# Ranking, placing and gathering the first expert's rows by row blocks, with the Exp table load behind the first weight slots, in a two-layer hybrid decoder trunk

## The chip, the cores and the metric

The kernel runs on one core of a Trainium2 chip. The metric is the device time of one execution in microseconds (us), taken as the median of several runs. Five engines work from queues of their own and wait for each other through semaphores: TensorE (PE, matmuls; PEld its weight loads), VectorE (DVE), ScalarE (ACT), GpSimd (POOL) and SyncE (SP, which here only issues the loads of weights).

## The reference, cut to what matters

```python
def rms_norm(x, g):
    xf = x.astype(jnp.float32)
    y = xf * lax.rsqrt(jnp.mean(xf * xf, axis=-1, keepdims=True) + NORM_EPS)
    return (y * g.astype(jnp.float32)).astype(x.dtype)

def moe_swiglu(h, w_router, w_gate, w_up, w_down):
    B, S, D = h.shape                      # 1, 256, 1024
    t = h.reshape(-1, D)
    logits = (t @ w_router).astype(jnp.float32)
    top_v, top_i = lax.top_k(logits, TOP_K)    # 2 of 8 experts
    top_w = jax.nn.softmax(top_v, axis=-1)
    combine = jnp.sum(jax.nn.one_hot(top_i, N_EXPERTS, dtype=jnp.float32) * top_w[..., None], axis=1)
    out = jnp.zeros_like(t)
    for e in range(N_EXPERTS):
        y = (jax.nn.silu(t @ w_gate[e]) * (t @ w_up[e])) @ w_down[e]
        out = out + combine[:, e:e + 1].astype(t.dtype) * y
    return out.reshape(B, S, D)

# each of two layers: x += concat(attention(h), conv(h)) @ w_out with h = rms_norm(x),
# then layer 0: x += dense_swiglu(rms_norm(x)), layer 1: x += moe_swiglu(rms_norm(x))
```

All data is float32. The sequence has 256 rows of 1024 numbers, an expert is 3584 wide.

## The kernel before

**Weights.** Every weight matrix is streamed in slots of 128 x 2048 numbers (1 MB). SP loads a slot into one of six buffers `raw`; ScalarE copies it to `w_high` in a shorter float format (`high(s)`), VectorE computes `w_low = raw - w_high` (`low(s)`), and TensorE multiplies in three terms (high by high, high by low, low by high; `terms`). `w_high` and `w_low` have three buffers each. So `high(s)` waits until slot s - 3 is used (`w_used`), and SP's load of slot s waits until the low part of slot s - 6 is done. The order of all this on each engine is written out by hand; there is no planner. An engine works strictly in that order.

**Rows.** The 256 rows are two blocks of 128 (NB = 2; b = 0, 1). `xr` holds them. `ps` is the accumulation memory, eight banks of 128 x 512.

**From layer 1's output projection to the first expert.** The last projection leaves its result in banks 4 to 7. VectorE adds it to `xr` in four halves (`add_rows`, counted by `x_added`), TensorE turns the rows (`turn_early`, `turn_rest`), ScalarE and VectorE copy the turned rows to `hT_plain` (`hT_plain_done`), and ScalarE squares the rows for the norm (`norm(3, (), split=False)`; `rms_done`). TensorE multiplies the turned rows with the router (`router(0, S)`, `router(1, P)`; four groups of columns side by side, whose sum is then made by `mm(..., lgT, mask)`), the rest of block 1 with plain matmuls, and signals `summed`. In `route` VectorE reads the logits (`lg`), compares every expert with every other (`cmp_a`), counts (`rank`) and picks the best two (`sel`, `sel_done`). TensorE counts by matmuls with a triangle (`tri`) and ones (`counted`). VectorE makes the place of each row (`possel`) and a one-hot tile `onehot[:, b, 0]` scaled with the row's norm factor (`onehot_done`). TensorE's `gather_first` multiplies `xr` with it: expert 0's rows come out turned, in banks 2, 3, 6 and 5. ScalarE copies them with the gain (`xg[0]`, `first_high_done`, L974), VectorE makes the low part in `first_low` (L1253). Then `gate_up(S_MOE, ...)` begins: slots 0 and 1 (counted from `S_MOE`) are the gate, 2 and 3 the up projection of 512 columns; slots 4 and 5 are the next columns' gate.

`fill(n, bank)` issues n matmuls of a zero tile whose results nobody reads. GpSimd's `list_tokens` makes the difference of the two best logits (`zdiff_done`), whose `Exp` gives the weights of the sum; they are read only in the last expert. `load_table(f)` runs a one-column activation of a function ahead of its use, so that the table of ScalarE changes there.

For VectorE the order of calls is `low(S_MOE)`, `norm_for_routing()`, `route()`, `low(S_MOE + 2)`, `first_low()`, `low(S_MOE + 3)`, `low(S_MOE + 4)`, `low(S_MOE + 5)`. The same stretch on ScalarE:

```python
norm(3, (), split=False)
high(S_MOE + 2)
load_table(ACT.Exp)
...   # eight copies of gathered rows, L974
act.activation(zt[:, :], zt[:, :], ACT.Exp).then_inc(z_done, 1)
load_table(ACT.Silu)
high(S_MOE + 3)
act.wait_ge(w_used, S_MOE + 2)
act.activation(silu_t, ps[:, 0, :], ACT.Silu).then_inc(silu_done, 1)
high(S_MOE + 4)
```

## Time and profile before

| | us |
|---|---|
| median of 3 runs | 1348.07 |
| lowest and highest of them | 1347.23, 1348.69 |
| the profiled execution | 1349.93 |
| its span, first to last instruction | 1348.3 |
| TensorE busy in it | 1339.0 |
| VectorE, ScalarE, GpSimd busy | 1102.8, 930.7, 123.7 |
| mean granted clock of TensorE | 0.999 of full |

The profile is of one execution. All times of a row are us from the start of its span, durations of single instructions are us too where nothing else is said. A timeline row gives start, duration, engine, line of the kernel, operation, result tile and operands, the shape, and how many instructions it joins (x); in brackets is the idle time ahead of it and what ended that. One matrix multiplication of float32 by float32 shows as two records, one in the shorter format as one. The ends of matmuls are modelled, and neighbours overlap.

### The profile page before, as it was taken

To read this page: it belongs to the slowest core of one execution; us is meant where nothing else is said; L and a number is where in the kernel's file an instruction comes from. 1 tells how busy PE (TensorE), PEld (TensorE's weight loads), DVE (VectorE), ACT (ScalarE), POOL (GpSimd) and SP (SyncE) were. 2 spreads that over 40 slices of the span, in tenths; PEclk is the share of its full clock that TensorE was granted. 3 is DMA by queue.
4 is the path that set the end of the run, shared out by engine and by line. 5 is a ranking of instruction groups with operands and counts; after the bars stand their busy time and mean duration, and the time that the engine had idled before them with its cause. 6 is when DMAs were issued, how large, how long until landed. Compare 5 with 4: busy or idle time off the path is not lost.

```text
span 1348.3 us, 17478 instructions
## 1 busy us (share of the span) xinstructions
PE 1339.0 (99%) x7287; PEld 1129.8 (84%) x7288; DVE 1102.8 (82%) x764; ACT 930.7 (69%) x785; POOL 123.7 (9%) x143
## 2 busy tenths in 40 slices
PE   9999999999999999999999999999999999999998
PEld 8879999999678888888888888888888888888886
DVE  6766555567768999998898889889888988988997
ACT  6675444465777777777777777777777777777774
POOL 4310000002045600000000000000000000000010
PEclk9999999999999999999999999999999999999999
DMA  9846555545459999999999999999999999999994
GB/s 318 243 136 207 183 185 184 185 144 189 144 193 337 395 394 381 395 374 374 392 386 361 391 394 367 372 392 393 371 377 396 370 368 394 389 365 376 397 396 173
DMA packets 200613, 430.79 MB, mean 319 GB/s; under 512 B 9752, under 2 KB 46256, under 8 KB 200528
## 3 DMA queue, kind: packets, MB, share of 16 engines
q1 hardware_dynamic: 195088, 415.37, 85.2%
q0 software_dynamic: 4576, 13.49, 2.7%
q8 instruction: 59, 0.97, 0.3%
q10 hardware_dynamic: 864, 0.74, 0.2%
q14 instruction: 26, 0.21, 0.0%
HBM read 417.56 MB, written 7.36 MB: 315 GB/s over the span
## 4 chain that ended last, share of the span: by engine, by line
PE 97%; DVE 1%; DMA 1%; SPq 0%; issue 0%; ACT 0%; DVEq 0%
PE ps L1426 94%; PE ps L1700 2%; PE ps L1452 1%; PE ps L1683 0%; DMA hT_both<-hpad 0%; DVE h_td L1206 0%; SPq L445 0%; DMA xr<-in_x 0%; DVE xr L1292 0%; DVE w_low L1017 0%; PE ps L1583 0%; PE ps L1549 0%; ACT cacc L790 0%; DVE xr L1058 0%; PE ps L1544 0%
## 5 line engine op out<-in xcount | busy, mean ns | idle before, releaser
L1017 DVE TENSOR_TENSOR w_low<-raw,w_high 128x2048 fp32r<-128x2048 f32 x387 | 892.5, 2307 | 161.7 <-ACT w_high L715 161.3
L715 ACT ACTIVATE w_high<-raw 128x2048 fp32r<-128x2048 f32 x389 | 745.4, 1917 | 283.6 <-PE ps L1426 283.6
L1426 PE MATMUL ps<-w_high,hT_both 128*128 128x512 f32 (+1 forms) x1920 | 600.0, 390 | 0.0
L1426 PEld LDWEIGHTS ps<-w_high,hT_both 128*128 128x128 f32 x1920 | 358.9, 188 | 71.9
L1426 PE MATMUL ps<-w_low,hT_both 128*128 128x512 f32 (+1 forms) x960 | 370.9, 386 | 0.0
L1426 PE MATMUL ps<-w_high,act_both 128*128 128x512 f32 x1072 | 342.6, 391 | 0.0
L1426 PEld LDWEIGHTS ps<-w_high,act_both 128*128 128x128 f32 x1072 | 201.4, 188 | 41.5 <-issue 0.3
L1426 PEld LDWEIGHTS ps<-w_low,hT_both 128*128 128x128 f32 x960 | 180.8, 188 | 34.9
L1426 PE MATMUL ps<-w_low,act_both 128*128 128x512 f32 x536 | 209.0, 390 | 0.0
L1426 PE MATMUL ps<-hT_both,w_high 128*128 128x256 f32 x960 | 176.9, 284 | 0.0
L1426 PEld LDWEIGHTS ps<-hT_both,w_high 128*128 128x128 f32 x960 | 151.3, 192 | 0.4
L1426 PE MATMUL ps<-hT_both,w_low 128*128 128x256 f32 x480 | 136.1, 283 | 0.0
L1426 PEld LDWEIGHTS ps<-w_low,act_both 128*128 128x128 f32 x536 | 100.8, 188 | 20.1
L1426 PEld LDWEIGHTS ps<-hT_both,w_low 128*128 128x128 f32 x480 | 92.2, 192 | 0.5
L682 POOL DMA_DIRECT2D y_slots<-work_a x7 | 4.1, 591 | 714.3 <-ACT work_a L935 714.3
L915 ACT ACTIVATE work_a<-ps 128x512 f32<-128x512 f32 x55 | 32.9, 599 | 40.0 <-PE ps L1426 40.0
L1298 DVE TENSOR_TENSOR act_both<-ps,act_both 128x512 fp32r<-128x512 f32 x56 | 38.3, 684 | 0.0
L1329 DVE TENSOR_TENSOR work_a<-ps,work_a 128x512 f32<-128x512 f32 x55 | 37.6, 683 | 0.0
L897 ACT ACTIVATE act_both<-ps 128x512 fp32r<-128x512 f32 x56 | 32.4, 578 | 2.4 <-PE ps L1700 2.4
L1700 PEld LDWEIGHTS ps<-ident,work_a 128*128 128x128 f32 x224 | 27.7, 138 | 7.3
L1700 PE MATMUL ps<-ident,work_a 128*128 128x128 f32 x224 | 33.5, 272 | 0.0
L562 POOL TENSOR_TENSOR gnorm<-mask,taps 128x1024 f32<-128x1024 f32 x4 | 11.7, 2935 | 211.3 <-DVE w_low L1017 201.1
(274 smaller groups left out, 684.1 us busy)
## 6 DMA issues: line engine op xcount, KB each, us to landing
raw<-in_moe_w_gate SPq DMA_DIRECT2D x112, 1024.0 KB, 8.7
raw<-in_moe_w_up SPq DMA_DIRECT2D x112, 1024.0 KB, 8.3
raw<-in_moe_w_down SPq DMA_DIRECT2D x112, 1024.0 KB, 8.2
raw<-in_w_in SPq DMA_DIRECT2D x13, 1024.0 KB, 6.9
raw<-in_dense_w_gate SPq DMA_DIRECT2D x11, 1024.0 KB, 6.0
raw<-in_dense_w_up SPq DMA_DIRECT2D x11, 1024.0 KB, 5.4
raw<-in_dense_w_down SPq DMA_DIRECT2D x11, 1024.0 KB, 4.9
raw<-in_w_out SPq DMA_DIRECT2D x8, 1024.0 KB, 7.0
```

The source lines that it names most:

```text
L562: pool.tensor_tensor(wconv[c], mask[:, :].unsqueeze(1).unsqueeze(1).to_broadcast([P, TG, 4, QUAD]), taps[:, l, :, c, :].unsqueeze(3).to_br ...
L682: pool.dma_start(y_dram[bass.ds(m * P, P), :], y_sb).then_inc(y_stored, 16)
L715: act.activation(w_part[0][:, s % PART_RING, :], raw[:, s % RAW_RING, :], ACT.Copy).then_inc(w_high_done, 1)
L897: act.activation(act_part[0][:, k % 2, :], ps[:, 2, :], ACT.Copy).then_inc(act_high_done, 1)
L915: act.activation(silu_t, ps[:, 0, :], ACT.Silu).then_inc(silu_done, 1)
L1017: dve.tensor_tensor(w_part[1][:, q, :], raw[:, r, :], w_part[0][:, q, :], ALU.subtract).then_inc(w_low_done, 1)
L1298: dve.tensor_tensor(act_part[1][:, k % 2, :], ps[:, 2, :], act_part[0][:, k % 2, :], ALU.subtract).then_inc(act_low_done, 1)
L1329: dve.tensor_tensor(prod_t, ps[:, 1, :], silu_t, ALU.mult).then_inc(prod_done, 1)
L1426: return pe.matmul(out_, lhsT, rhs, start=start, stop=stop, skip_group_check=True)
L1452: last = pe.transpose(turned(k)[:, b * P:(b + 1) * P], xr[:, b, k * P:(k + 1) * P], ident[:, :])
L1700: last = pe.transpose(ps[:, 2, f * P:(f + 1) * P], prod_t[:, f * P:(f + 1) * P], ident[:, :])
```

## The change

The routing is done block by block. TensorE multiplies `router(1, P)` ahead of `turn_rest(3)`, sums block 0's logits alone into bank 0 (`summed` 1), block 1's into bank 5 (`summed` 2), counts block 0 alone in bank 4 and block 1 in bank 7, and gathers in three pieces: half of block 0's part, the other half behind block 1's counting, then block 1's part. Eight fills go and three come. VectorE ranks block 0, reads the logits of block 1, places block 0 (one-hot tile), ranks block 1 and places it. ScalarE copies `lgT` ahead of the last copy of `hT_plain`. `first_low()` comes ahead of `low(S_MOE + 2)` on VectorE. On ScalarE `load_table(ACT.Exp)`, which stood ahead of the copies of the gathered rows, stands behind them, and `high(S_MOE + 3)` ahead of it, where it stood behind `Exp` and the load of `Silu`'s table. The same values are computed.

```diff
--- before.py
+++ after.py
@@ -764,10 +764,10 @@
                 act.wait_ge(x_added, 4 * (q - 1) + 3)
                 act.activation(h_td[:, 1, 0:D // 2], xr[:, 1, 0:D // 2], ACT.Square, accum_out=ss[:, q, 1:2]).then_inc(sq_done, 1)
                 if not split:
+                    act.wait_ge(routed, 1)
+                    act.activation(lgT, ps[:, 4, 0:S], ACT.Copy).then_inc(lgT_ready, 1)
                     act.wait_ge(h_turned, KC // 2 * q + 3)
                     act.activation(hT_plain[:, 4:8:2, P:S], late_turned(0)[:, :, P:S], ACT.Copy).then_inc(hT_plain_done, 1)
-                    act.wait_ge(routed, 1)
-                    act.activation(lgT, ps[:, 4, 0:S], ACT.Copy).then_inc(lgT_ready, 1)
                 act.wait_ge(sq_done, done + 2)
                 act.activation(ss_half[:, q, 0:1], ss[:, q, 1:2], ACT.Identity, scale=1.0 / D, bias=eps_t[:, :]).then_inc(sq_done, 1)
                 if split:
@@ -966,7 +966,6 @@
                 high(S_MOE + j)
             norm(3, (), split=False)
             high(S_MOE + 2)
-            load_table(ACT.Exp)
             for k in range(KC):
                 act.wait_ge(first_gathered, 2 * (k // 4) + k % 2 + 1)
                 if k % 4 > 1:
@@ -974,10 +973,11 @@
                 act.activation(xg[0][:, k, 0, :], first_rows(k), ACT.Copy, scale=gcols[:, GAIN[3] + k:GAIN[3] + k + 1]).then_inc(first_high_done, 1)
             act.wait_ge(first_high_done, KC)
             act.sem_inc(xg_high_done, 2)
+            high(S_MOE + 3)
+            load_table(ACT.Exp)
             act.wait_ge(zdiff_done, 1)
             act.activation(zt[:, :], zt[:, :], ACT.Exp).then_inc(z_done, 1)
             load_table(ACT.Silu)
-            high(S_MOE + 3)
             act.wait_ge(w_used, S_MOE + 2)
             act.activation(silu_t, ps[:, 0, :], ACT.Silu).then_inc(silu_done, 1)
             high(S_MOE + 4)
@@ -1220,31 +1220,44 @@
 
             def route():
 
-                dve.wait_ge(summed, 1)
+                def read_logits(b):
+
+                    dve.wait_ge(summed, b + 1)
+                    link(dve.tensor_copy(lg[:, b, :], ps[:, (0, 5)[b], 0:NE]))
+
+                def rank_block(b):
+
+                    mine = lg[:, b, :].unsqueeze(2).to_broadcast([P, NE, NE])
+                    other = lg[:, b, :].unsqueeze(1).to_broadcast([P, NE, NE])
+                    link(dve.tensor_tensor(cmp_a[:, b], other, mine, ALU.subtract))
+                    link(dve.tensor_tensor(cmp_a[:, b], cmp_a[:, b], tie8[:, :, :], ALU.is_gt))
+                    link(dve.tensor_reduce(rank[:, b, :], cmp_a[:, b], AX.X, ALU.add))
+                    dve.tensor_scalar(sel[:, b, :], rank[:, b, :], 2.0, None, ALU.is_lt).then_inc(sel_done, 1)
+
+                def place_block(b):
+
+                    dve.wait_ge(counted, b + 1)
+                    dve.wait_ge(sel_done, b + 1)
+                    link(dve.scalar_tensor_tensor(out=possel[:, b, :], in0=ps[:, (4, 7)[b], 0:NE], scalar=1.0,
+                                                  in1=sel[:, b, :], op0=ALU.add, op1=ALU.mult))
+                    dve.scalar_tensor_tensor(out=onehot[:, b, 0], in0=iota_c[:, :], scalar=possel[:, b, 0:1],
+                                             in1=rstd[:, 3, b:b + 1].to_broadcast([P, P]), op0=ALU.is_equal, op1=ALU.mult).then_inc(onehot_done, 1)
+
                 dve.wait_ge(rank_tiles, 2)
-                link(dve.tensor_copy(lg[:, :, :], ps[:, 5, 0:NB * NE].rearrange("p (b e) -> p b e", b=NB)))
-                mine = lg[:, :, :].unsqueeze(3).to_broadcast([P, NB, NE, NE])
-                other = lg[:, :, :].unsqueeze(2).to_broadcast([P, NB, NE, NE])
-                link(dve.tensor_tensor(cmp_a[:, :, :, :], other, mine, ALU.subtract))
-                link(dve.tensor_tensor(cmp_a[:, :, :, :], cmp_a[:, :, :, :], tie8[:, :, :].unsqueeze(1).to_broadcast([P, NB, NE, NE]), ALU.is_gt))
-                link(dve.tensor_reduce(rank[:, :, :], cmp_a[:, :, :, :], AX.X, ALU.add))
-                dve.tensor_scalar(sel[:, :, :], rank[:, :, :], 2.0, None, ALU.is_lt).then_inc(sel_done, 1)
+                read_logits(0)
+                rank_block(0)
+                read_logits(1)
+                place_block(0)
+                rank_block(1)
                 dve.wait_ge(rms_done, 8)
                 link(dve.reciprocal(rstd[:, 3, 1:2], rms[:, 3, 1:2]))
-                dve.wait_ge(counted, 1)
-                dve.wait_ge(sel_done, 1)
-                link(dve.scalar_tensor_tensor(out=possel[:, :, :], in0=ps[:, 4, 0:NB * NE].rearrange("p (b e) -> p b e", b=NB), scalar=1.0,
-                                              in1=sel[:, :, :], op0=ALU.add, op1=ALU.mult))
-                for b in range(NB):
-                    dve.scalar_tensor_tensor(out=onehot[:, b, 0], in0=iota_c[:, :], scalar=possel[:, b, 0:1],
-                                             in1=rstd[:, 3, b:b + 1].to_broadcast([P, P]), op0=ALU.is_equal, op1=ALU.mult).then_inc(onehot_done, 1)
+                place_block(1)
                 for r in range(2):
                     link(dve.tensor_scalar(selr[:, r], rank[:, :, :], float(r), None, ALU.is_equal))
                 dve.sem_inc(ranked, 1)
                 dve.tensor_copy(row_factor[:, :, :], rstd[:, 3, :].unsqueeze(2).to_broadcast([P, NB, 8])).then_inc(rstd_done, 1)
-                dve.wait_ge(counted, 2)
-                dve.tensor_copy(counts[:, 0:NB, :], ps[:, 4, 0:NB * NE].rearrange("p (b e) -> p b e", b=NB))
-                dve.tensor_copy(counts[:, NB, :], ps[:, 7, 0:NE]).then_inc(counts_copied, 1)
+                dve.tensor_copy(counts[:, 0, :], ps[:, 4, 0:NE])
+                dve.tensor_copy(counts[:, 1:NB + 1, :], ps[:, 7, 0:2 * NE].rearrange("p (b e) -> p b e", b=NB)).then_inc(counts_copied, 1)
 
             def first_low():
 
@@ -1383,8 +1396,8 @@
             low(S_MOE)
             norm_for_routing()
             route()
+            first_low()
             low(S_MOE + 2)
-            first_low()
             low(S_MOE + 3)
             low(S_MOE + 4)
             low(S_MOE + 5)
@@ -1655,16 +1668,14 @@
                         last.then_inc(half_projected, 1)
                 last.then_inc(w_used, 1)
 
-            def gather_first():
-
-                for n in range(4):
-                    for b in range(NB):
-                        if n == 0:
-                            pe.wait_ge(onehot_done, b + 1)
-                        for k in (4 * (n // 2) + n % 2, 4 * (n // 2) + n % 2 + 2):
-                            last = mm(first_rows(k), xr[:, b, k * P:(k + 1) * P], onehot[:, b, 0, :], k % 4 < 2 and b == 0, b == 1)
-                    last.then_inc(first_gathered, 1)
-                pe.sem_inc(gathered, 2)
+            def gather_first(b, ns):
+
+                pe.wait_ge(onehot_done, b + 1)
+                for n in ns:
+                    for k in (4 * (n // 2) + n % 2, 4 * (n // 2) + n % 2 + 2):
+                        last = mm(first_rows(k), xr[:, b, k * P:(k + 1) * P], onehot[:, b, 0, :], k % 4 < 2 and b == 0, b == 1)
+                    if b == NB - 1:
+                        last.then_inc(first_gathered, 1)
 
             def gather(i, per, e, e_reg):
 
@@ -1818,27 +1829,29 @@
             pe.wait_ge(hT_plain_done, 2)
             router(0, S)
             pe.wait_ge(hT_plain_done, 4)
+            router(1, P).then_inc(routed, 1)
             turn_rest(3)
-            router(1, P).then_inc(routed, 1)
-            fill(1, 7)
+            pe.wait_ge(lgT_ready, 1)
+            mm(ps[:, 0, 0:NE], lgT[:, 0:P], mask[:, 0:NE], True, True).then_inc(summed, 1)
+            mm(ps[:, 5, 0:NE], lgT[:, P:S], mask[:, 0:NE], True)
             pe.wait_ge(hT_plain_done, 6)
             for k in range(4, KC):
-                mm(ps[:, 5, NE:2 * NE], hT_plain[:, k, P:S], wr[:, k, 0:NE], k == 4)
-            pe.wait_ge(lgT_ready, 1)
-            for t in range(NB):
-                last = mm(ps[:, 5, t * NE:(t + 1) * NE], lgT[:, t * P:(t + 1) * P], mask[:, 0:NE], False, True)
+                last = mm(ps[:, 5, 0:NE], hT_plain[:, k, P:S], wr[:, k, 0:NE], False, k == KC - 1)
             last.then_inc(summed, 1)
-            fill(5, 7)
             pe.wait_ge(pool_consts, 12)
             pe.wait_ge(rank_tiles, 1)
             pe.wait_ge(sel_done, 1)
-            mm(ps[:, 4, 0:NE], tri[:, :], sel[:, 0, :], True, True)
-            mm(ps[:, 4, NE:2 * NE], tri[:, :], sel[:, 1, :], False)
-            mm(ps[:, 4, NE:2 * NE], ones_b[:, :], sel[:, 0, :], False, True).then_inc(counted, 1)
-            mm(ps[:, 7, 0:NE], ones_b[:, :], sel[:, 0, :], True)
-            mm(ps[:, 7, 0:NE], ones_b[:, :], sel[:, 1, :], False, True).then_inc(counted, 1)
-            fill(2, 0)
-            gather_first()
+            mm(ps[:, 4, 0:NE], tri[:, :], sel[:, 0, :], True, True).then_inc(counted, 1)
+            fill(3, 7)
+            gather_first(0, range(2))
+            pe.wait_ge(sel_done, 2)
+            mm(ps[:, 7, 0:NE], tri[:, :], sel[:, 1, :], True)
+            mm(ps[:, 7, 0:NE], ones_b[:, :], sel[:, 0, :], False, True)
+            mm(ps[:, 7, NE:2 * NE], ones_b[:, :], sel[:, 0, :], False)
+            mm(ps[:, 7, NE:2 * NE], ones_b[:, :], sel[:, 1, :], False, True).then_inc(counted, 1)
+            gather_first(0, range(2, 4))
+            gather_first(1, range(4))
+            pe.sem_inc(gathered, 2)
             gate_up(S_MOE, 0, None, 0, arriving=True)
             pe.wait_ge(silu_done, DG + 1)
             gate_up(S_MOE + 4, 0, None, 0, ms=(0,))
```

## Rows read from the trace of the kernel before

**Rows 1.** The page: span, and TensorE's busy time with its share and instructions.
```profile
span 1348.3 us, 17478 instructions
PE 1339.0 (99%) x7287; PEld 1129.8 (84%) x7288; DVE 1102.8 (82%) x764; ACT 930.7 (69%) x785; POOL 123.7 (9%) x143
```

**Rows 2.** Waits, 470 to 1330: who for whom, total us, times, longest.
```profile
ACT w_high L715 <- PE ps L1426: 163.8, 235, 1.1
```

**Rows 3.** Waits of SP's queue, 392 to 1330, same columns.
```profile
SPq L407 <- DVE w_low L1017: 802.1, 327, 7.9
```

**Rows 4.** Chain of waits, 360 to 480: start, us, engine, tile, line.
```profile
382.54 0.63 PE ps L1452 x4
...
385.29 0.19 DVE lg L1225
...
386.47 0.18 DVE sel L1231
...
387.31 0.36 DVE work_b L1239
...
387.71 20.23 PE ps L1426 x104
```

**Rows 5.** Timeline of TensorE, 370 to 420.
```profile
381.60 0.64 PE L1426 MATMUL ps<-work_a,wr 128*32 128x256 f32 x8
...
383.10 0.43 PE L1426 MATMUL ps<-work_a,wr 128*32 128x128 f32 x8
...
383.79 0.95 PE L1426 MATMUL ps<-wr,work_a 128*128 128x8 f32 x8
...
387.71 3.84 PE L1426 MATMUL ps<-work_b,xr 128*128 128x128 f32 x32
391.31 0.49 PE L1426 MATMUL ps<-w_high,hT_both 128*128 128x512 f32 x1
...
407.78 0.60 PE L1700 MATMUL ps<-ident,work_a 128*128 128x128 f32 x4
```

**Rows 6.** Timeline of ScalarE, 366 to 440.
```profile
382.99 0.38 ACT L768 ACTIVATE work_a<-ps 128x256 f32<-128x256 f32 x1 [0.64 <-PE ps L1452]
...
386.91 1.28 ACT L797 ACT_TABLE_LOAD   x1
...
393.36 0.20 ACT L978 ACTIVATE zt<-zt 128x2 f32<-128x2 f32 x1
393.58 1.28 ACT L797 ACT_TABLE_LOAD   x1
...
394.98 1.90 ACT L715 ACTIVATE w_high<-raw 128x2048 fp32r<-128x2048 f32 x1
397.10 0.60 ACT L982 ACTIVATE work_a<-ps 128x512 f32<-128x512 f32 x1 [0.21 <-PE ps L1426]
397.59 1.91 ACT L715 ACTIVATE w_high<-raw 128x2048 fp32r<-128x2048 f32 x1
399.88 1.92 ACT L715 ACTIVATE w_high<-raw 128x2048 fp32r<-128x2048 f32 x1 [0.38 <-PE ps L1426]
```

**Rows 7.** Timeline of VectorE, 366 to 440.
```profile
383.21 0.42 DVE L1097 COPY work_a<-ps 128x256 f32<-128x256 f32 x1 [0.81 <-PE ps L1452]
...
385.82 0.29 DVE L1229 TENSOR_TENSOR cmp_a<-cmp_a,tie 128x128 f32<-128x128 f32 x1
...
388.60 2.28 DVE L1017 TENSOR_TENSOR w_low<-raw,w_high 128x2048 fp32r<-128x2048 f32 x1
390.80 0.60 DVE L1253 SCALAR_TENSOR_TENSOR hT_both<-ps,gcols,hT_both 128x128 fp32r<-128x128 f32 x2
...
399.53 4.59 DVE L1017 TENSOR_TENSOR w_low<-raw,w_high 128x2048 fp32r<-128x2048 f32 x2 [0.32 <-ACT w_high L715]
```

**Rows 8.** Timeline of GpSimd, 366 to 440: the operand of `Exp`.
```profile
392.47 0.20 POOL L592 TENSOR_TENSOR zt<-zt,rstd 128x2 f32<-128x2 f32 x1
```

**Rows 9.** TensorE by stretches: us, busy (records), granted clock, DMA share, GB/s.
```profile
382.20:386.80 4.60, 3.97 (x35) 1.00 0.78 221
...
1342.50:1348.30 5.80, 0.07 (x1) 0.78 0.46 163
```

## Prediction

> **What bounds the kernel now.** I read the page first [rows 1]: TensorE is busy for 1339.0 of 1348.3 us. Busy is not proof of a bound, so the waits of the experts' part come next: there the longest list is ScalarE waiting for a matmul to free a part slot, 163.8 us in 235 waits [rows 2], and no wait of TensorE stands above it. The weight queue waits only for `w_low`, that is for a free raw slot [rows 3], never the other way round. So from 391 us on TensorE runs at its own pace, and a microsecond by which the experts' matmuls start sooner is a microsecond off the end, unless something in between makes TensorE wait again.
>
> The stretch that the change rebuilds lies between the last projection of layer 1 and the first expert matmul. The chain of waits shows it as one thread that hops over the engines [rows 4]: `turn_rest` at 382.54, logits copied at 385.29, `sel` at 386.47, the one-hot tile at 387.31, and from 387.71 on only matmuls. TensorE's timeline [rows 5] splits these: 32 gather records in 3.6 us up to 391.31, where the first expert matmul starts, then 72 expert matmuls to the turn at 407.78. 407.78 - 391.31 = 16.47 us, or 0.2288 us each; a part slot holds 12 of them, so a slot lasts 2.745 us. Slot 4 (I count from `S_MOE`) starts at 391.31 + 4 x 2.745 = 402.29.
>
> **How tight the supply is.** A slot must pass ScalarE (high part) and VectorE (low part), and the high part of slot s waits until slot s - 3 is used. ScalarE [rows 6]: `Exp` at 393.36, table load for `Silu` at 393.58, high of slot 3 at 394.98, `Silu` at 397.10, high of slot 4 at 397.59. VectorE [rows 7]: lows of slots 4 and 5 together from 399.53, 4.59 us, so slot 4 is ready at about 401.8, 0.5 us ahead of 402.29. That 0.5 us is the number to keep in mind: slot 4 is nearly late already.
>
> **The change, part 1: the routing.** Times are those of this profile.
> - Router and logits. `router(0)` starts at 381.60 and issues for about 0.45 us [rows 5]; `router(1)` now follows at once instead of behind `turn_rest`, so `routed` comes at about 382.5 rather than 383.5 (end of the row at 383.10). ScalarE's `lgT` copy (0.38 us, as its neighbour of the same shape in [rows 6]) ends at 382.95. `turn_rest` stays where it is, 382.54, since it waits for the rows of `x`; the copy at 382.99 that was ahead of `lgT` stays at 383.0. The first block's sum issues at 383.05 and ends at 383.45.
> - Block 0 ranked. VectorE is in its copy at 383.21 (0.42 us) and a reciprocal until 383.70 [rows 7]; so `lg` of block 0 is read at 383.73. Before, the read began 385.29. A step on 128 elements takes 0.29 us and one on 16 takes 0.18 [rows 4, 7]; halved tiles of 64 and 8 elements lie between, I take 0.22 and 0.165. Read, three steps and `sel` with a 0.03 us link each: 0.20 + 3 x 0.25 + 0.17 = 1.12, `sel` of block 0 at 384.85. Then one matmul and the link back: before, `sel`'s end at 386.65 to the one-hot at 387.31 took 0.66; with one counting matmul instead of three ahead of it 0.55, so one-hot 0 runs from 385.40 to 385.75. The three fills (0.69 us at 0.2288) end at 385.8. Gather of half of block 0: 8 records at 0.113 = 0.9, to 386.72.
> - Block 1. Its matmuls on 4 plain tiles still wait for VectorE's copy at 383.63, so they run at 383.79 as before (0.95 us), `lg` 1 is read at 384.8, inside a wait that VectorE has anyway. `rank_block(1)` follows one-hot 0: 385.65 + 3 x 0.25 + 0.17 gives `sel` at 386.59. TensorE's four small matmuls run at 386.73 to 386.85; one-hot 1 is ready at 387.60. Meanwhile TensorE gathers the rest of block 0 until 387.8, then block 1's 16 records, 1.8 us, to 389.6.
> - `first_low` ahead of slot 2's low. In [rows 7] slot 2's low (2.28 us from 388.60) delays the first low gather to 390.80. In the new order ScalarE's first high runs at about 388.5, the low at 388.9 to 389.25, so it is ready before the gather ends. The eight pairs alternate until 391.5 (high) and 391.9 (low), each ahead of the matmul that wants it, 0.69 us apart. Slot 2's low then runs 391.9 to 394.2, wanted at 389.6 + 5.5 = 395.1: covered, by 0.9 us. The raw slot that it frees is refilled 3.3 us later than now; SP would wait at 394.2 instead of 390.9, and that load is wanted only after 409.
>
> So the first expert matmul moves from 391.31 to about 389.6: a gain of 1.7 us at this place. Bounds: 389.3 with every link at its shortest, 390.3 if block 1's chain is 0.5 to 0.7 us longer than its rows and the gather waits for it.
>
> **Part 2: the table load.** Now ScalarE does high 2, the `Exp` table, eight copies, `Exp`, the `Silu` table, high 3, `Silu`, high 4. After the change: eight copies, high 3, `Exp` table, `Exp`, `Silu` table, `Silu`, high 4. The load at 386.91 lay in time in which ScalarE would have waited for the gather, and so cost nothing; this cover is given up. High 3 can't fill the time at 391.5 either: it waits until slot 0 is used. From the row at 397.10, `Silu` follows the matmul start that ends its slots by 0.3, and high 5 follows its by 0.4, so with G for the first expert matmul high 3 starts at G + 2.745 + 0.37 = G + 3.12. From there, by [rows 6]: high 1.91, load with its warm-up 1.40 (393.58 to 394.98), `Exp` 0.22 (393.36 to 393.58), load 1.40, `Silu` 0.49 (397.10 to 397.59), high 4 up to its low 1.94 (397.59 to 399.53). Low 4 takes 2.28 and 0.1 to TensorE. Sum: G + 3.12 + 1.91 + 1.40 + 0.22 + 1.40 + 0.49 + 1.94 + 2.28 + 0.10 = G + 12.86. `Exp`'s operand is ready at 392.7 [rows 8] and needs no wait. TensorE would be at slot 4 at G + 10.98. **It waits 1.9 us there.** With G = 389.6 slot 4 starts at 402.46, against 402.29 now: the 1.7 us won are given back, and 0.2 on top. Behind it: low 5 ends at 404.6, wanted at 405.2; the product at 405.3, wanted at 407.95; high 6 needs slot 3's end, which is past; low 6 ends at 407.5, wanted at 408.3. No further wait, and none is made good, since TensorE has no slack.
>
> A rule speaks against more: the Trainium skill ("ScalarE: Activation LUTs", What ACT_TABLE_LOAD costs) gives a switch of tables about 2.66 us, 1.28 of load and 1.38 of drain. This case's trace shows 0.22 from `Exp` to the load and 1.40 for load and warm-up, no drain of that length [rows 6]; by the page two switches would cost 5.3 and the sum would be 2.5 us more. I take the row.
>
> **Sum.** +0.2 us against the profile's span. The profiled execution took 1349.93 us, 1.6 around its span, and is 1.9 above the median of the three runs; a difference carries over: 1348.07 + 0.2 = 1348.3 us. With G at 389.3 or 390.3 it is -0.1 or +0.9, and I allow 0.3 for the links of the ScalarE chain: own range 1347.7 to 1349.3.
>
> **Rivals.**
> - *The forecast, slot 4 late by the two table loads*: 0.58, 1348.3.
> - *The gather isn't ahead.* Block 1's chain (`sel`, count, `possel`, one-hot) outlasts block 0's gather by a us or more, because half tiles cost nearly as much as whole ones and there are twice as many links. For it: 0.18 us for 16 elements, 0.29 for 128, so the fixed part is most of the price. Against it: the count above leaves 0.2 us of cover and each step was priced from such rows. G = 390.6 to 391.3, then + 12.86: +1.2 to +1.9, 1349.6. Chance 0.13.
> - *The gain stays.* The wait at slot 4 doesn't appear, because ScalarE reaches high 4 sooner than I sum. It would take 1.9 us out of a chain of recorded durations. -1.7: 1346.4. Half of it is as likely as all of it. Chance 0.15.
> - *TensorE's clock falls* (the slower side). Fills go from eight to three and TensorE then waits 1.9 us in one piece, right behind the start. In the stretch of now the granted clock is 1.00, its level of 2.4 GHz, through eight fills [rows 9]. After the last matmul the mean over 5.8 us is 0.78: half of full for 2.6 us, so it had held for about 3 us of nothing before it fell to 1.2 GHz. A wait of 1.9 us is shorter; that speaks against it. It decides if the thinner stretch at 382 to 386 and the wait count together: then the gather's 3.6 us take twice as long and some expert slots too, +3.6 to +6: 1352.5. Chance 0.10. A rule says the same: the Trainium skill ("TensorE: Matmul & The Clock Gate", What's actually happening) has the half-rate clock as the state of an idle engine.
> - Otherwise, the page's drain among it: +2.5, 0.04.
>
> **Numbers.** A measurement of this kernel tells 0.2% (2.7 us) from no change. Only the clock and the drain, in their upper part, reach over it: slower 0.06. Faster by 2.7 us is more than all that the change could win: 0.02. Within 0.2%: 0.92. The range leaves out the clock case and the tips of the others, and holds 0.85 of the chance with the 0.7 us by which the three runs scatter: 1346.3 to 1350.0 us.
>
> **What the profile would show.** First expert matmul near 389.6 (step 1 right), or at 391 (gather rival). Two table loads on ScalarE between 394.5 and 397.7, none in 386 to 389. TensorE idle 1.9 us at 400.5, ended by `w_low`, slot 4 at 402.5; if that wait is missing, the gain stays. Granted clock below 1.00 between 384 and 404 for the clock rival. I would be wrong above all if a link that I price at 0.03 to 0.15 us grew in the half-size form, or if the load and the copies behind it overlap.

## The result, and the profile after

The changed kernel takes 1354.45 us (median of 6 runs, 1351.61 to 1356.68) against 1347.82 for the kernel before (6 runs); the ratio is 1.0043, 95% interval 1.0033 to 1.0053. In a second series of 10 runs it took 1351.89 against 1347.97, ratio 1.0022 (1.0012 to 1.0032). So it is 4 to 6.6 us slower where 1348.3 us was forecast, and its runs scatter over 5 us. Its profiled execution took 1356.68 us, its span is 1355.1.

The stretch ahead of the change ends at another time in each profile (`turn_rest` starts at 379.7 to 383.7 us in all of them, in the kernel before at 382.54 [rows 4]). To compare stretches I count from landmarks: X, the start of `turn_rest`; G, the first expert matmul; t1 and t2, the first and second turn of a product; and the end of the span. Before: G - X = 8.77, t1 - G = 16.47, t2 - t1 = 11.53, end - t2 = 928.99.

TensorE's timeline of the changed kernel, beside [rows 4, 5]:

```profile
383.65 0.66 PE L1465 MATMUL ps<-ident,xr 128*128 128x128 f32 x4
...
386.16 0.17 PE L1439 MATMUL ps<-sel,tri 128*128 128x8 bf16 x1 [0.28 <-DVE sel L1235]
386.18 1.24 PE L1439 MATMUL ps<-w_high,zero_r 128*128 128x512 f32 x3
387.22 1.92 PE L1439 MATMUL ps<-work_b,xr 128*128 128x128 f32 x8
...
389.08 3.39 PE L1439 MATMUL ps<-work_b,xr 128*128 128x128 f32 x24
392.22 0.48 PE L1439 MATMUL ps<-w_high,hT_both 128*128 128x512 f32 x1
...
405.12 0.47 PE L1439 MATMUL ps<-w_high,hT_both 128*128 128x512 f32 x1 [1.74 <-DVE w_low L1017]
...
410.66 0.60 PE L1711 MATMUL ps<-ident,work_a 128*128 128x128 f32 x4
...
422.22 0.60 PE L1711 MATMUL ps<-ident,work_a 128*128 128x128 f32 x4
424.70 0.47 PE L1439 MATMUL ps<-w_high,hT_both 128*128 128x512 f32 x1 [1.88 <-DVE w_low L1017]
```

Three things are to be read. Half of block 0's gather, 8 records, lasts 1.92 us, where the sum had 0.9; G - X is 8.57 instead of 7.06. Slot 4 waits 1.74 us, near the 1.9 of the sum; t1 - G is 18.44. And there is a wait that the sum didn't have, 1.88 us at 424.7, the first of several: end - t2 is 932.88. The parts are -0.20, +1.97, +0.03 (t2 - t1) and +3.89, in all 5.69 us; the other 1.1 us of the two spans' difference is X itself, 383.65 against 382.54. That lies ahead of the change: the router's matmuls, with which the changed stretch begins, already start 1.2 us later (382.80 against 381.60 [rows 5]).

The gather first. TensorE by stretches, columns as in [rows 9]:

```profile
384.00:387.00 3.00, 2.67 (x19) 0.94 0.95 250
387.00:390.00 3.00, 3.00 (x17) 0.50 0.72 274
390.00:393.00 3.00, 3.00 (x26) 0.99 0.03 3
```

From about 386.6 to 390.0 the granted clock is 0.50, 1.2 GHz. Before it fell TensorE had done matmuls of 8 columns and waited 0.28 us for `sel`.

Then the late wait. The chain of waits of the changed kernel passes through a load of `w_down` for 16.81 us, where that of before had only matmuls; and ScalarE's timeline shows that it waits for loads already ahead of that. The third block is what it waited for landings in all, from 392 to 1340 (total us, times, longest):

```profile
418.74 16.81 DMA raw<-in_moe_w_down
```

```profile
420.31 1.92 ACT L715 ACTIVATE w_high<-raw 128x2048 fp32r<-128x2048 f32 x1 [4.26 <-DMA raw<-in_moe_w_gate]
423.69 1.91 ACT L715 ACTIVATE w_high<-raw 128x2048 fp32r<-128x2048 f32 x1 [1.46 <-DMA raw<-in_moe_w_gate]
426.45 1.92 ACT L715 ACTIVATE w_high<-raw 128x2048 fp32r<-128x2048 f32 x1 [0.84 <-DMA raw<-in_moe_w_up]
```

```profile
ACT w_high L715 <- DMA raw<-in_moe_w_gate: 8.9, 6, 4.3
ACT w_high L715 <- DMA raw<-in_moe_w_up: 3.8, 5, 1.5
ACT w_high L715 <- DMA raw<-in_moe_w_down: 2.8, 3, 1.9
```

ScalarE waits 4.26 us for a weight slot to land; before, its waits were for matmuls [rows 2]. SP's queue and VectorE show what is issued later than before, GpSimd what the loads meet:

```profile
397.04 2.91 SPq L407 DMA_DIRECT2D raw<-in_moe_w_down  x2
405.00 2.57 SPq L407 DMA_DIRECT2D raw<-in_moe_w_gate  x2
```

```profile
391.56 2.17 DVE L1266 SCALAR_TENSOR_TENSOR hT_both<-ps,gcols,hT_both 128x128 fp32r<-128x128 f32 x6 [0.93 <-ACT hT_both L973]
...
394.72 2.29 DVE L1017 TENSOR_TENSOR w_low<-raw,w_high 128x2048 fp32r<-128x2048 f32 x1
```

```profile
394.53 2.57 POOL L597 TENSOR_TENSOR place_b<-selr,place_a 128x16 f32<-128x16 f32 x2
397.17 2.45 POOL L582 TENSOR_TENSOR place_b<-place_b 128x16 f32<-128x16 f32 x2
...
400.76 1.10 POOL L603 DMA_INDIRECT slot_tokens<-tok_i,list_i  x1 [0.61 <-POOL list_i L599]
```

```profile
402.00:404.00 2.00, 1.53 (x2) 1.00 0.98 400
404.00:406.00 2.00, 1.80 (x1) 1.00 0.04 11
406.00:408.00 2.00, 1.89 (x1) 1.00 2.01 55
408.00:410.00 2.00, 0.01 (x1) 1.00 0.21 28
410.00:412.00 2.00, 0.00 (x0) 1.00 0.34 39
```

Slot 2's low part runs at 394.72, 11.1 us behind X (before 388.60, 6.1 behind), so its raw slot is refilled from 397.04 on. GpSimd's steps at L597 and L582 lie over VectorE's low parts and take 2.5 us for two, and the four scatters of the token list start at 400.76, 17.1 us behind X (before 13.1). The last block is of the stretches of GpSimd (busy time and count are its own; the last columns are the clock, the DMA share and GB/s): from 404 to 412 the DMA engines move 11 to 55 GB/s, with one gate slot of 1 MB outstanding from 405, a second from 407 and a third load issued at 410.

The refill and the first scatter in the kernel before:

```profile
390.91 8.69 SPq L407 DMA_DIRECT2D raw<-in_moe_w_down  x2
```

```profile
395.63 1.10 POOL L603 DMA_INDIRECT slot_tokens<-tok_i,list_i  x1 [0.61 <-POOL list_i L599]
```

The last number of the rows below is the time from issue to landing of one load: the first two gate slots of the changed kernel (issued from 405.00), then those of before (from 401.85).

```profile
raw<-in_moe_w_gate SPq DMA_DIRECT2D x1, 1024.0 KB, 15.3
raw<-in_moe_w_gate SPq DMA_DIRECT2D x1, 1024.0 KB, 16.5
```

```profile
raw<-in_moe_w_gate SPq DMA_DIRECT2D x1, 1024.0 KB, 8.0
raw<-in_moe_w_gate SPq DMA_DIRECT2D x1, 1024.0 KB, 11.5
```

So the refill that is issued later isn't itself slow: it lands after 4.9 us. The loads behind it are. And the kernel before has the same collision, only milder: its loads slow down beside the scatters too (45 GB/s from 412 to 414), but ScalarE never has to wait for one.

### The profile page after: what moved, and what is told of

It reads as the page before. It is cut to its first block, busy times and chain, and to the rows that moved or that the text cites. A ratio compares the mean times of both kernels' runs of the same rounds, so it can differ in the third digit from the quotient of the medians.

```text
span 1355.1 us, 17474 instructions
## 1 busy us (share of the span) xinstructions
PE 1340.4 (99%) x7282; PEld 1129.8 (83%) x7283; DVE 1104.1 (81%) x770; ACT 930.7 (69%) x785; POOL 125.2 (9%) x143
## 4 chain that ended last, share of the span: by engine, by line
PE 95%; DMA 2%; DVE 1%; ACT 1%; SPq 0%; issue 0%; DVEq 0%; ACTq 0%
PE ps L1439 91%; PE ps L1711 2%; DMA raw<-in_moe_w_down 1%; PE ps L1465 1%; DVE w_low L1017 1%; ACT w_high L715 1%; PE ps L1694 0%; DMA hT_both<-hpad 0%; DVE h_td L1206 0%; DMA xr<-in_x 0%; SPq L445 0%; DVE xr L1305 0%; ACT L797 0%; PE ps L1596 0%; PE ps L1562 0%
```

## The experiments

All comparisons are with the kernel before, run on the same chip, 10 to 12 timed runs of each kernel and 33 to 35 of before (in the first series, row "changed", 6 of each). The kernels without scatters compute other values, since the token list is missing. Columns: clock, the mean granted clock from X to G; the three stretches of the profile; "sum", (end - X) less the 965.76 of before; "landing", what ScalarE waited for weight slots to land from 392 to 1340 us; last, the difference of the medians and the ratio's interval.

| kernel | clock | G - X | t1 - G | end - t2 | sum | landing | median | ratio, 95% |
|---|---|---|---|---|---|---|---|---|
| before | 1.00 | 8.77 | 16.47 | 928.99 | 0 | 0 | 0 | |
| changed | 0.80 | 8.57 | 18.44 | 932.88 | +5.69 | 15.5 | +6.6 | 1.0033-1.0053 |
| after_again | 0.81 | 8.76 | 18.43 | 931.99 | +4.96 | 14.3 | +3.9 | 1.0012-1.0032 |
| t_only | 1.00 | 8.78 | 18.46 | 929.04 | +2.06 | 0 | +2.3 | 1.0004-1.0022 |
| l_only | 1.00 | 8.77 | 16.47 | 930.33 | +1.35 | 11.2 | +1.1 | 0.9998-1.0015 |
| r_only | 0.82 | 9.55 | 16.43 | 928.97 | +0.73 | 0.9 | +0.7 | 0.9991-1.0009 |
| r_t | 0.83 | 9.92 | 18.43 | 928.98 | +3.10 | 0.9 | +3.6 | 1.0011-1.0029 |
| r_l | 0.80 | 8.75 | 16.47 | 932.24 | +3.26 | 13.1 | +2.6 | 1.0002-1.0023 |
| after_fills | 1.00 | 7.32 | 18.45 | 929.00 | +0.57 | 5.8 | +0.6 | 0.9995-1.0012 |
| after_nolist | 1.00 | 7.16 | 18.44 | 929.44 | +0.83 | 0 | +1.9 | 0.9999-1.0017 |
| l_nolist | 1.00 | 8.78 | 16.44 | 929.37 | +0.35 | 0 | +0.6 | 0.9994-1.0012 |
| after_nofill | 0.80 | 8.75 | 18.50 | 929.83 | +2.86 | 11.8 | +2.6 | 1.0009-1.0027 |
| nofill_nolist | 0.80 | 8.64 | 18.48 | 929.42 | +2.32 | 0 | +2.4 | 1.0010-1.0029 |
| r_l_fills | 1.00 | 7.31 | 16.46 | 931.70 | +1.27 | 12.4 | +1.2 | 1.0003-1.0021 |
| r_l_fills_nolist | 1.00 | 7.32 | 16.45 | 929.30 | -1.14 | 0 | -1.4 | 0.9978-0.9996 |
| list_first | 1.00 | 7.32 | 16.45 | 929.30 | -1.16 | 9.8 | -0.8 | 0.9987-1.0005 |
| r_fills | 1.00 | 8.80 | 16.43 | 928.78 | -0.22 | 0 | -0.3 | 0.9988-1.0006 |
| before_list_first | 1.00 | 8.77 | 16.44 | 929.94 | +0.93 | 11.1 | +1.4 | 1.0006-1.0024 |

The sums of the single profiles agree with the medians within 1.1 us, so I read causes from the stretches and sizes from both. Two single executions far off (3466.66 and 2722.59 us, after_again and nofill_nolist) don't move the medians.

The last stretch can be split at the turns of the later products. What the changed kernel loses behind t2 it has lost by the second turn behind it, 34 us on: 3.94 us, and no more up to the last turn, about 915 us behind t2. In the four kernels without scatters this part is 0.01 us or less at every turn; their 0.3 to 0.5 us in the table come behind the last product, from a source that isn't known.

**t_only**: ScalarE's order alone, on the kernel before.

```diff
             high(S_MOE + 2)
-            load_table(ACT.Exp)
...
             act.sem_inc(xg_high_done, 2)
+            high(S_MOE + 3)
+            load_table(ACT.Exp)
...
             load_table(ACT.Silu)
-            high(S_MOE + 3)
```

> The kernel before with one edit alone: ScalarE's order as in the change (high part of slot 3 ahead of the Exp table load, which stands behind the copies of the gathered rows). Theory A (two table loads stand between the high part of slot 3 and Silu, so slot 4 is late): the first expert matmul stays at 391.3 of the span, slot 4 starts 12.9 us behind it instead of 11.0, TensorE idle 1.9 us there; +1.9 us in all, or some tenths more if the refills of raw slots slip too. Rival (the loads are hidden, the loss of the change is all from elsewhere): no idle time at slot 4, 0.0 us.

Theory A holds: t1 - G is 18.46, 2.0 us more, with 1.74 us of TensorE idle ahead of slot 4, and nothing behind it.

**l_only**: VectorE's order alone.

```diff
-            low(S_MOE + 2)
             first_low()
+            low(S_MOE + 2)
```

> The kernel before with one edit alone: the low parts of the gathered rows ahead of slot 2's low part on VectorE. Theory B (the load that refills slot 2's raw buffer is issued later, the DMA engines stand idle meanwhile and the stream of weights, which needs nearly all of their rate, never catches up): slot 2's low part at about 393.5, the next load of w_down at 395.8 instead of 390.9, ScalarE waits for landings between 410 and 460, +1 to +3 us. Rival (that load is wanted only much later, as predicted): ScalarE waits for matmuls alone, -0.3 to 0.0 us.

Theory B: the load of `w_down` is issued 13.1 us behind X instead of 8.4 (393.11), and ScalarE waits 11.2 us for landings where it waited for none. The profile loses 1.34 us behind t2; the medians differ by 1.1 us, with an interval that just holds no change. Two things stand beside it. The gate loads are issued 19.3 us behind X in both kernels, so the stream as a whole is not behind. And the same edit moves the scatters as well: they start 14.3 us behind X instead of 13.1, since one of GpSimd's steps now lies beside VectorE's low part.

**r_only**: the routing alone (the changed kernel with both moves undone).

> The change without its two moves on ScalarE and VectorE: only the routing by row blocks (slot 2's low part ahead of the low gather, Exp's table load where it was). Theory C (with fewer fills TensorE's clock falls for some 3 us in the routing, so that the first expert matmul comes no earlier): granted clock under 0.9 between 385 and 391, first expert matmul within 0.5 us of 391.3, -0.5 to +1.5 us. Rival (the clock matters little, the routing by blocks saves its time): start at 390 to 390.8, -1.0 us.

The clock falls (0.82). G - X is 9.55, worse than I had set for theory C, since the low gather waits again for slot 2's low part (TensorE idle 0.68 us ahead of G). No gain, no clear loss.

**after_fills**: the changed kernel with three fills more.

```diff
             mm(ps[:, 5, 0:NE], lgT[:, P:S], mask[:, 0:NE], True)
+            fill(1, 7)
             pe.wait_ge(hT_plain_done, 6)
...
             last.then_inc(summed, 1)
+            fill(2, 7)
```

> The changed kernel with three fills more, in places where TensorE waits anyway (one ahead of block 1's plain logits, two behind them). Theory C: the granted clock stays at 1.00 through the routing, the first expert matmul comes 1.5 us earlier than in the changed kernel and the runs scatter less, but the wait at slot 4 and the late landings stay: about 1.5 us less than the changed kernel, +3 to +5 us against before. Rival (the clock is the whole loss): within 1 us of before.

The clock stays at 1.00 and G - X falls to 7.32. But the total fell by more than the 1.5 us of theory C: end - t2 is 929.00 in this profile, and the median is +0.6. That is the number of the rival (within 1 us of before) and a miss for theory C. The rival's reason doesn't hold, though: the wait at slot 4 is still there (t1 - G 18.45), the start gains 1.45 us, and the two nearly cancel. So three fills took away 3 to 6 us, more than the clock itself costs.

**after_again**: the changed kernel once more.

> The changed kernel itself, once more beside the others, since its six runs scatter over 5 us. Both theories: +4 to +7 us against before, first expert matmul 8.6 us behind turn_rest, slot 4 12.9 us behind that. If the extra 3.9 us behind the second turn are a chance collision of transfers, its profile can lack them and its runs scatter again over some 5 us; if they follow from the order of the work, they are there in each.

All parts recur, 3.0 us behind t2 among them; runs from 1349.3 to 1354.1.

**after_nolist**: the changed kernel without the scatters.

```diff
-                for b in range(NB):
-                    for r in range(2):
-                        pool.indirect_dma_start(out=slot_dram[:, :], out_offset=bass.IndirectOffsetOnAxis(ap=list_i[:, r, b:b + 1], axis=0),
-                                                in_=tok_i[:, b:b + 1], in_offset=None).then_inc(tokens_listed, 16)
-                pool.wait_ge(tokens_listed, 16 * 2 * NB)
```

> The changed kernel without the four scatters that write the token list (so the list that is read back is all zeros, and experts 1 to 6 get row 0 throughout). Theory D (in the changed kernel the weight loads, issued late, run into the scatters and get hardly any bandwidth meanwhile): the loads land in time, no wait of TensorE behind the first turn, the 3.9 us there are gone: +1 to +2 us against before, from slot 4's wait alone. Rival E (the late refill alone starves the stream): still +4 to +6 us.

No landing is waited for; 2.0 us less than after_again beside it. But in this one profile the clock stayed at 1.00 with the same three fills, so it doesn't separate scatters from clock. Its runs (1347.9 to 1351.8) would fit a clock that falls in some and not in others; that is inferred.

**r_t**: the changed kernel with VectorE's order of before. **r_l**: with ScalarE's order of before.

> The change without the new place of the low gather on VectorE (slot 2's low part ahead of it, as before): routing by blocks and the table load as in the change. Late refill theory (B): nothing lands late, so what is left is the routing with its clock (0.7 us by its own profile) and the wait at slot 4 (1.9): +2 to +3 us. Rival (order on VectorE is harmless): as the changed kernel, +4 to +7 us.

> The change without the move on ScalarE (Exp's table load ahead of the copies, high part of slot 3 behind Silu's load): routing by blocks and the low gather first. Theory B: slot 2's low part late, loads land late, +1 to +4 us with a clock fall in the routing. Rival (only the two tables behind the first rows cost, or the clock): 0 to +1 us.

r_t lands in time (end - t2 928.98) and pays for the tables (18.43) and a late start (9.92: clock, and 1.12 us of waiting for the low gather); its median is 0.6 us above my range. r_l has no wait at slot 4 (16.47) and loses 3.25 us behind t2. The parts add up for r_t (0.73 + 2.06 against 3.10 in the profiles), but not for r_l (0.73 + 1.35 against 3.26), nor for all three (4.14 against 5.69): the surplus lies behind t2, where the loss varies between executions.

**l_nolist**: l_only without the scatters. **after_nofill**: the changed kernel without `fill(3, 7)`. **nofill_nolist**: both left out.

> The kernel before with the low gather first on VectorE, and without the four scatters that write the token list (experts 1 to 6 get row 0 throughout). Theory D (late loads collide with the scatters): the 1.3 us that the low gather first cost behind the second turn are gone, ScalarE waits for no landing, end 929.0 us behind the second turn as before: 0.0 us. Rival E (the late refill alone starves the stream): ScalarE still waits for landings, 930.3, +1 us.

> The changed kernel without its three fills. Theory C (a routing too thin in matmuls drops TensorE's clock in some executions, and that makes the scatter of the runs): now it falls in nearly every one, the first expert matmul is 8.6 us or more behind turn_rest, and the runs lie at the upper end of the changed kernel's, +4 to +6 us, with less scatter. Rival (the fills do nothing or only cost time): as the changed kernel or less, +2 to +4 us.

> The same without the four scatters as well (experts 1 to 6 get row 0 throughout). Theory D: granted clock still low in the routing, but the 3 to 4 us behind the second turn are gone: the end 929 to 930 us behind it, +3 us against before at most. Rival E: 932 to 933 us behind it, as in the changed kernel.

Without scatters no landing is waited for, whatever the clock: 929.37 and 929.42 behind t2. That decides for D against E: the late refill alone doesn't starve the stream. In the medians these two pairs show no difference (+1.1 against +0.6, +2.6 against +2.4). after_nofill misses its expectation and meets the rival's: the clock falls, but it loses only 0.84 us behind t2 and its median, +2.6, is no more than the changed kernel's. The three fills at their place, behind the first count, change nothing that I can measure.

**r_l_fills**: after_fills with ScalarE's order of before.

> The version that the runs so far point to: routing by blocks with six fills and the low gather first, ScalarE's order as in the kernel before (Exp's table load ahead of the copies). Theory A with C: clock 1.00, first expert matmul 7.3 us behind turn_rest instead of 8.8, and slot 4 at most 0.5 us late, since one table load less stands ahead of Silu: -1.0 us if the loads land in time, 0 to +1 if they don't. Rival (the gain at the start is given back at slot 4 in any order): 0 us or more.

The start is 1.46 us better, slot 4 isn't late at all (I had allowed 0.5), and all of it goes behind t2 (931.70). +1.2 us, a miss on the upper side. This is what left D open in the full routing, and led to four more.

**r_l_fills_nolist**: the same without the scatters. **list_first**: the same, with the scatters, ahead of two small stores.

```diff
-            pool.wait_ge(rstd_done, 1)
-            for b in range(NB):
-                pool.dma_start(h_dram[b * P:(b + 1) * P, D:D + 8], row_factor[:, b, :]).then_inc(h_stored, 16)
             list_tokens()
...
+                pool.wait_ge(rstd_done, 1)
+                for b in range(NB):
+                    pool.dma_start(h_dram[b * P:(b + 1) * P, D:D + 8], row_factor[:, b, :]).then_inc(h_stored, 16)
                 pool.wait_ge(tokens_listed, 16 * 2 * NB)
```

> Routing by blocks with six fills, low gather first, ScalarE's order as before, without the four scatters of the token list (experts 1 to 6 get row 0 throughout). Theory D: nothing lands late, the 2.7 us behind the second turn are 0.4 as in the other kernels without scatters, and the 1.45 us of the start stay: -1.0 us against before. Rival E (the late refill alone): +1 us as with the scatters.

> Routing by blocks with six fills, low gather first, ScalarE's order as before, and GpSimd computes and scatters the token list ahead of its two small stores of the row factors, so that it is through before VectorE's low parts slow it. Theory D: the scatters start at 11 us behind turn_rest instead of 16, while the weight stream is idle, the late loads meet less of them: 0 to 1 us lost behind the second turn instead of 2.7, -1.0 to 0.0 us against before. Rival: the scatters last into the loads anyway, +1 us.

The stream of r_l_fills and that of the kernel without scatters, 23 to 35 and 24 to 36 us behind X (SP's stretches; last column GB/s):

```profile
405.00:408.00 3.00, 1.00 1.43 248
408.00:411.00 3.00, 1.00 0.66 44
411.00:414.00 3.00, 1.00 0.78 256
414.00:417.00 3.00, 1.00 1.35 217
```

```profile
407.00:410.00 3.00, 1.00 1.04 382
410.00:413.00 3.00, 1.00 1.03 380
413.00:416.00 3.00, 1.00 1.06 417
416.00:419.00 3.00, 1.00 1.02 401
```

Without scatters the loads, issued just as late, keep 380 to 417 GB/s, and the kernel is 1.4 us faster than before (0.9978 to 0.9996), though without a token list: the start's gain comes through. With the list's scatters at 12.5 instead of 16.2 us behind X the loss behind t2 goes from 2.71 to 0.31 us in the profile, and the median from +1.2 to -0.8 (0.9987 to 1.0005, so it is not shown to beat the kernel before). ScalarE still waits 9.8 us for landings, in waits that TensorE hardly feels; and since that loss varies between executions of one order, one profile doesn't show that the list's new place removed it. In the diff the added lines stand in `list_tokens`, behind the scatters.

**r_fills**: routing alone with six fills. **before_list_first**: GpSimd's edit alone, on the kernel before.

> Routing by blocks alone with six fills; slot 2's low part ahead of the low gather and ScalarE's order as before. Theory C: clock 1.00; the gather ends 7.3 us behind turn_rest, but the first low gather waits for slot 2's low part, so the first expert matmul is 8.3 to 8.7 us behind; nothing lands late: -0.4 to 0.0 us. Rival (the start gains its 1.45 us even so): -1.4 us.

> The kernel before with the one edit on GpSimd alone (token list ahead of the two stores of the row factors). Control: no load is late there, so nothing to win: within 0.3 us of before. If it gains as much as list_first does, the collision costs the kernel before too.

r_fills is as theory C has it, with the start 0.1 us later: the gather is done, and TensorE waits 1.23 us for the low gather behind slot 2's low part, G - X 8.80. The control came out otherwise than either side: 1.4 us slower, 11.1 us of landings waited for, with its load of `w_down` in time at 8.4 us behind X and its scatters at 12.8, hardly moved. So loads can run into GpSimd's small transfers without a late refill.

## Why the prediction was wrong, by its steps

**What bounds the kernel.** Right that time saved at the start is time saved at the end: r_l_fills_nolist turns 1.45 us of start into 1.4 of median. But I read from SP's waits [rows 3] that the loads have room. That row says that they were always in time, not by how much.

**Routing, 1.7 us won: right in mechanism, and only where the clock holds.** With it G - X is 7.16 to 7.32 for the forecast 7.06. I took the gather's records at 0.113 us each; the clock is where this step failed in the changed kernel. Of eight profiles with the new routing and three fills or none, seven have a mean clock of 0.80 to 0.83 from X to G; of five with six fills all have 1.00. It costs 1.3 to 1.6 us (8.57 to 8.76 against 7.16 to 7.32). My clock rival had a chance of 0.10; it came true, but ahead of the wait at slot 4 and not because of it, and at 1.4 us where I had priced 3.6 to 6. The row that I held against it (about 3 us of nothing at the end of the kernel) did not carry over to a stretch of short matmuls and waits.

**The table loads: right.** Wait of 1.9 us forecast, 1.74 recorded, t1 - G 1.97 longer, in every kernel with that order and in none without. The Trainium skill's 2.66 us for a switch ("ScalarE: Activation LUTs", What ACT_TABLE_LOAD costs) isn't what this trace shows: load, warm-up and next activation stand at 397.25, 398.54 and 398.65, 1.40 us.

```profile
397.25 1.28 ACT L797 ACT_TABLE_LOAD   x1
398.54 0.20 ACT L797 ACTIVATE warm<-eps_t 128x1 f32<-128x1 f32 x1
398.65 0.19 ACT L979 ACTIVATE zt<-zt 128x2 f32<-128x2 f32 x1
398.86 1.28 ACT L797 ACT_TABLE_LOAD   x1
```

**"The raw slot that it frees is refilled 3.3 us later ... and that load is wanted only after 409": the step that failed.** I priced it at nothing because that one load is in time, which it was. But the gate and up loads behind it already shared the DMA engines with the token list before, and now take longer: the two gate loads 15.3 and 16.5 us to land instead of 8.0 and 11.5. All seven profiles with the late refill and the scatters at their old place wait 5.8 to 15.5 us for landings, and end - t2 is 0.0 to 3.9 us over before; the four without scatters wait for none and lose at most 0.01 us up to the last product; the five with the old order (before, t_only, r_only, r_t, r_fills) wait for 0 to 0.9 and are within 0.3. This term, 3.9 us in the profile of the changed kernel and 3.0 in its repeat, is most of what the sum lacked; the clock is the rest. I counted SP's refill and asked who waits for that load; I did not ask what else is in flight by then, nor saw that GpSimd's list is slower while VectorE makes low parts. Which of the two makes the collision worse isn't separated: the new place of the low part moves both the refill (13.1 instead of 8.4 us behind X in l_only) and the scatters (14.3 instead of 13.1). For the refill speaks r_t, whose scatters start at 14.3 too, with the refill at 9.5, and which loses nothing behind t2; against it as the only cause before_list_first, which loses 0.95 us with neither of them late.

Why the clock rival and this one came as a pair, so that six fills saved 3 to 6 us, isn't settled: after_nofill has the low clock and loses only 0.84 us behind t2, r_l_fills has the full clock and loses 2.71. The loss varies between executions of one order.

**What stays open.** That the scatters are needed for the waits on landings and for the loss behind t2 is shown in the profiles of four kernels by taking them out; in the medians only one pair shows it clearly (r_l_fills with +1.2 us, without scatters -1.4). Why four scatters of 128 four-byte numbers can hold loads of 1 MB at 35 GB/s for 7 us (405 to 412) isn't; nor what sets the size between 0 and 3.9 us; nor why two stores of 4 KB behind the scatters cost the kernel before 1.4 us.

## What to carry to other kernels

Where a weight stream needs nearly all of the DMA engines' rate, a buffer freed later can cost time even if the load into it is in time: before moving the instruction that frees it, look at what else will be in flight when the load starts, and at which other engine's work the move shifts. Price a table load by what stands behind it in the queue, not by where the engine looked idle; there the old place, in a wait of ScalarE, was free. And when fills around a sparse stretch are removed, read the granted clock of several executions: a profile in which it held (one of eight here) proves nothing.

## What the runs showed of the hardware that I had not expected

- The granted clock fell to 0.50 in a stretch in which TensorE had instructions nearly all the time: busy 8.24 of 8.57 us from X to G, mean 0.80. Ahead of the fall were matmuls of 8 columns, eight of them in 1.06 us, and a wait of 0.28 us for `sel`. With three more 512-column fills ahead of the counting it stayed at 1.00 in five of five profiles.
- A two-operand step of GpSimd on 16 numbers takes 0.22 us alone and up to 2.27 us beside VectorE's low part of a slot. In the changed kernel L597 is 2.57 us for two, in r_fills, where no slot's low part runs beside it, 0.52 for the same two. The Trainium skill says that the two engines share their SBUF interfaces ("GPSIMD Engine Reference", Key points), with contention when VectorE reads two SBUF inputs; these rows agree. By it the token list, and with it the scatters, move when a low part is moved.

```profile
392.15 0.52 POOL L597 TENSOR_TENSOR place_b<-selr,place_a 128x16 f32<-128x16 f32 x2
```

- GpSimd goes on from the scatters, which it starts 17.1 us behind X in the changed kernel, only 20 us later (400.76 to 420.53); the two loads of `w_up` issued from 410 took 16.4 and 16.7 us to land, against 11.5 for the same two in the kernel before and 8.3 in the median of all its loads of `w_up`.
